# The first block of a two-block model as one program block: rows normalised after the projection, attention in the order three-branch, latent, banded

## What is computed

```python
def hybrid_layer(x, w_in, w_out, g_pre, g_post, ...):
    h = rms_norm(x, g_pre)
    a_q, a_kv, a_g, b_cq, b_ckv, b_kr, c_q, c_kv, z = split_cols(h @ w_in)
    o_a = nsa_attention(a_q, a_kv, a_g, cmp_pos, cmp_w1, cmp_w2, rel_bias[:4])
    qb = rms_norm(b_cq, q_norm) @ w_uq          # latent heads, rotary part added
    kvb = rms_norm(b_ckv, kv_norm) @ w_ukv
    o_b = causal_block_attention(q_full, k_full, v, scale)
    o_c = banded_attention(c_q, c_k, c_v, 128, rel_bias[4:], sinks)
    mixed = concatenate([o_a, o_b, o_c]) * silu(z)
    return x + rms_norm(mixed @ w_out, g_post)
```

## Time and profile before

| What | us |
|---|---|
| Median of three runs | 2661.77 (2660.51 to 2672.22) |
| The profiled execution | 2659.23, its span 2657.4 |
| First product of the input projection, layer 0 | 41.0 |
| Attention, layer 0 | 199.5 to 299.8 |
| Output projection, layer 0, last tile done | 353.5 |
| Input projection, layer 1, third tile starts | 395.0 |
| Second block's first instruction | 715.4 |

### The profile page before, as it was taken

How to read it: one execution, slowest core, us unless ns; L and a number is a source line. 1 busy time by engine, 2 the same in 40 slices (tenths; PEclk the granted TensorE clock), 3 DMA queues, 4 the chain that set the end, 5 groups by cost and what they waited for, 6 DMA issues and landing times. The chain is left out here.

```text
span 2657.4 us, 35733 instructions
## 1 busy us (share of the span) xinstructions
PE 2513.5 (95%) x13328; PEld 2002.8 (75%) x13328; DVE 1274.9 (48%) x1879; ACT 685.4 (26%) x1365; POOL 673.9 (25%) x516
## 2 busy tenths in 40 slices
PE   7999879998799999999899999899999999999997
PEld 4875558765488888787688888688887887788886
DVE  4446454465443334586733344433344876533344
ACT  2126431165221110354311110311100642311101
POOL 1006430064233321200433311233311101433311
PEclk9999989998899999998999999899999999999999
DMA  5310123200322332230233332233322321233322
GB/s 205 95 56 1 41 94 98 69 1 17 102 87 95 99 111 91 72 97 25 87 100 98 95 113 89 64 95 97 112 99 72 96 65 56 83 99 95 116 98 75
DMA packets 57556, 223.35 MB, mean 84 GB/s; under 512 B 6696, under 2 KB 7848, under 8 KB 57056
## 3 DMA queue, kind: packets, MB, share of 16 engines
q1 hardware_dynamic: 56000, 213.97, 25.0%
q10 hardware_dynamic: 1440, 7.79, 0.8%
HBM read 219.59 MB, written 2.15 MB: 83 GB/s over the span
## 5 line engine op out<-in xcount | busy, mean ns | idle before, releaser
L171 DVE CAST two_hi<-two_raw 128x1024 fp32r<-128x1024 f32 (+1 forms) x292 | 219.8, 753 | 907.6 <-PE bank L240 897.1
L233 PE MATMUL bank<-xh,two_hi 128*128 128x512 f32 x1728 | 429.8, 391 | 0.1
L240 PE MATMUL bank<-xl,two_hi 128*128 128x512 f32 x1728 | 427.5, 389 | 0.0
L236 PE MATMUL bank<-xh,two_lo 128*128 128x512 f32 x1728 | 426.8, 389 | 0.0
L173 DVE TENSOR_TENSOR two_lo<-two_raw,two_hi 128x1024 fp32r<-128x1024 f32 (+1 forms) x292 | 400.9, 1373 | 10.0
L236 PEld LDWEIGHTS bank<-xh,two_lo 128*128 128x128 f32 x1728 | 324.4, 188 | 67.6
L240 PEld LDWEIGHTS bank<-xl,two_hi 128*128 128x128 f32 x1728 | 324.4, 188 | 67.2
L233 PEld LDWEIGHTS bank<-xh,two_hi 128*128 128x128 f32 x1728 | 322.9, 188 | 68.6 <-issue 1.4
L1464 POOL TENSOR_TENSOR up_hm<-up_sg,up_hm 128x512 f32<-128x512 f32 x88 | 197.5, 2244 | 555.9 <-ACT up_hm L1446 555.9
L233 PE MATMUL bank<-hh,two_hi 128*128 128x512 f32 x704 | 171.8, 392 | 0.0
L240 PE MATMUL bank<-hl,two_hi 128*128 128x512 f32 x704 | 171.4, 390 | 0.0
(11 more groups left out here) (318 smaller groups left out, 3131.9 us busy)
## 6 DMA issues: line engine op xcount, KB each, us to landing
two_raw<-in_up SPq DMA_DIRECT2D x180, 512.0 KB, 3.5
two_raw<-in_down SPq DMA_DIRECT2D x64, 704.0 KB, 4.0
one_raw<-in_w_in SPq DMA_DIRECT2D x52, 512.0 KB, 3.6
two_raw<-in_w_in SPq DMA_DIRECT2D x40, 512.0 KB, 3.6
one_raw<-in_w_out SPq DMA_DIRECT2D x16, 512.0 KB, 3.5
two_raw<-in_w_out SPq DMA_DIRECT2D x16, 512.0 KB, 3.7
w<-in_w ACTq DMA_DIRECT2D x2, 2048.0 KB, 10.5
x<-in_x SPq DMA_DIRECT2D x1, 2048.0 KB, 8.3
```

The lines of the kernel that those rows point to most:

```text
L171: v.tensor_copy(st.hi[:, h, 0:w], st.raw[:, r, 0:w]).then_inc(st.hi_made, 1)
L233: pe.matmul(out[:], st.hi[:, slot, k * P:(k + 1) * P], xh[:, h * kp + k, :], start=h == 0 and k == 0, stop=False)
L236: pe.matmul(out[:], st.lo[:, slot, k * P:(k + 1) * P], xh[:, h * kp + k, :], start=False, stop=False)
L240: mm = pe.matmul(out[:], st.hi[:, slot, k * P:(k + 1) * P], xl[:, h * kp + k, :], start=False, stop=h == pieces - 1 and k == kp - 1)
```

## The change

- **One block.** `first_block` writes out both layers for each engine, without barriers or a loop; the loads of SyncE too (`fetch_first`).
- **Start.** x comes in four pieces with two weight tiles between. The distance rows are made after the first two tiles. Of the four far rows (4 × 1,024) and eight near rows (8 × 384) 128 copies each go to DRAM (`store_bias`, after the load of weight tile 7), and `read_bias`, after the load of tile 11, reads them back with a row step one shorter than the row, so that no turning is needed. `biasK` is gone: compressed keys read every sixteenth element of `biasA`.
- **Norm.** `xh` and `xl` are made of x times the gain, without the root. ScalarE squares x afterwards, VectorE adds the squares, TensorE sums them after tile 3, and VectorE multiplies with the root as it moves each tile out of PSUM (`evict`). Tiles 0 to 5 have six banks. SiLU is then a step of its own on ScalarE.
- **Attention.** The 24 three-branch pairs come first, then 8 latent, then 16 banded. At steps 17 and 20 VectorE splits the first two tiles of the output projection; in the last steps ScalarE (`convert`) and then GpSimd make `xh` and `xl` of the mixed rows.
- **Output projection.** Eight banks hold the result. ScalarE squares from PSUM, VectorE scales in place and adds to x, and layer 1 takes chunks of x as they are made. No second sum of squares is made here.

```diff
-            sp.dma_start(kit.x[:], d["x"]).then_inc(s["x_loaded"], 16)
-            kit.stream.start(sp)
-            sp.dma_start(d["scratch"], vec[:]).then_inc(s["stored"], 16)
...
-            sp.dma_start(ha[:], bass.AP(src.tensor, src.offset, [[1, P], [2 * T, A_HEADS], [1, 896]])
...
+def fetch_first(sp, st, n):
+    sp.dma_start(st.raw[:, u, :], src[at:at + 1].rearrange("o p k -> (o p) k")).then_inc(st.w_loaded[u], 16)
...
+        for i in range(4):
+            sp.dma_start(kit.x[:, 2 * i:2 * i + 2, :], d["x"][:, 2 * i:2 * i + 2, :]).then_inc(s[f"x_in{i}"], 16)
+            if i < 2:
+                fetch_first(sp, st, i)
...
+    def store_bias(sp):
+        sp.wait_ge(s["vec_made"], 3)
+        sp.dma_start(d["far"], first.vec[0:A_HEADS].unsqueeze(1).to_broadcast([A_HEADS, P, 2 * T])
+                     ).then_inc(s["stored"], 16)
+        sp.dma_start(d["near"], first.near[:].unsqueeze(1).to_broadcast([C_HEADS, P, NEAR_W])).then_inc(s["stored"], 16)
+    def read_bias(sp):
+        sp.wait_ge(s["stored"], 32)
+        for dst, name, sem, heads, w, n in ((kit.biasC, "near", "read_c", C_HEADS, NEAR_W, 256),
+                                            (kit.biasA, "far", "read_a", A_HEADS, 2 * T, BIAS_W)):
+            src = d[name]
+            sp.dma_start(dst[:], bass.AP(src.tensor, src.offset + P - 1, [[w - 1, P], [w * P, heads], [1, n]])
+                         ).then_inc(s[sem], 16)
...
 def attention_pairs():
+    for c in range(2):
+        for n in reversed(range(NT)):
+            for b, kind in enumerate(("cmp", "slc", "win")):
+                add(kind, c, n, (2 * c, 2 * c + 1), branch=b, first=b == 0, last=b == 2)
+    for c in range(2):
+        for n in reversed(range(NT)):
+            add("mla", 2 + c, n, (2 * c, 2 * c + 1), first=True, last=True)
-    for c in range(4):
-        for n in reversed(range(NT)):
-            add("swa", 4 + c, n, (2 * c, 2 * c + 1), first=True, last=True)
...
-    return (0, 4)[i % 2]
+SPLIT_AT = (17, 20)
+TILES = (0, 1, 2, 3, 4, 5, 6, 7)
+IN_BANKS = (0, 4, 1, 2, 6, 7)
+Y_BANKS = (0, 4, 1, 2, 6, 7, 3, 5)
+XSUM_BANK = 3
+    return IN_BANKS[i] if i < len(IN_BANKS) else IN_BANKS[(i - len(IN_BANKS)) % 4]
...
-            a.activation(kit.xrstd[:], kit.xsum[:], ACT.Ln, bias=kit.eps[:, 0:1], scale=1.0 / D).then_inc(s["ln_made"], 1)
-                a.activation(kit.xh[:, c, :], hn[:, c, :], ACT.Copy).then_inc(s["xhi_made"], 1)
-                v.scalar_tensor_tensor(hn[:, c, :], kit.x[:, c, :], kit.gpre[:, c:c + 1], kit.xrstd[:],
-                                       ALU.mult, ALU.mult).then_inc(s["hn_made"], 1)
+            gain = kit.gains[:, 0, l, c:c + 1]
+            a.activation(kit.xh[:, c, :], kit.x[:, c, :], ACT.Copy, scale=gain).then_inc(s["xhi_made"], 1)
+            a.activation(hn[:, c, :], kit.x[:, c, :], ACT.Copy, scale=gain).then_inc(s["hn_made"], 1)
+        for c in range(DC):
+            a.activation(xsq[:, c, :], kit.x[:, c, :], ACT.Square).then_inc(s["xsq_made"], 1)
+        a.dma_start(s1[:], d["s1"][l]).then_inc(s["s1_in"], 16)
...
+        a.activation(kit.xrstd[:], bank[XSUM_BANK][:], ACT.Ln, bias=kit.eps[:, 0:1], scale=1.0 / D
+                     ).then_inc(s["ln_made"], 1)
...
-            def evict(i):
-                a.wait_ge(st.mm_done, st.done_after(l, base + i))
-                a.activation(proj[:, i, :], bank[dense_bank(i)][:], ACT.Silu if i < C_Z + DC else ACT.Copy,
-                             scale=HD ** -0.5 if i in SCALED else 1.0).then_inc(s["out_taken"], 1)
+        def evict(i):
+            v.wait_ge(st.mm_done, n0 + i + 1 + HL_RING)
+            if i == 0:
...
+            if i in SCALED:
+                out = v.scalar_tensor_tensor(proj[:, i, :], src, HD ** -0.5, kit.xrstd[:], ALU.mult, ALU.mult)
+            else:
+                out = v.tensor_tensor(proj[:, i, :], src, kit.xrstd[:], ALU.mult)
+            out.then_inc(s["taken"], 1)
...
+                for c in range(1, DC):
+                    v.wait_ge(s["xsq_made"], c + 1)
+                    if c > 1:
+                        v.wait_ge(s["xsq_added"], c - 1)
+                    v.tensor_tensor(xsq[:, 0, :], xsq[:, 0, :], xsq[:, c, :], ALU.add).then_inc(s["xsq_added"], 1)
+            if i == 3:
+                for e in range(3):
+                    evict(e)
+            if i >= 3:
+                evict(i)
...
+            if j in SPLIT_AT:
+                split(N_IN + SPLIT_AT.index(j))
...
+        convert_at = {NU - 4: (0, 1), NU - 3: (2, 3), NU - 2: (4,), NU: (5,), NU + 1: (6,)}
+        def convert(p):
+            a.wait_ge(s["turned"], groups_of[NU - L_RING + p // 2][-1] + 1)
+            a.wait_ge(s["mixed"], p + 1)
+            a.activation(kit.xh[:, p, :], rows_of(p), ACT.Copy).then_inc(o["xhi_made"], 1)
...
+        for p in range(DC):
+            g.wait_ge(s["turned"], groups_of[NU - L_RING // 2 + p // 2][-1] + 1)
+            g.wait_ge(o["xhi_made"], p + 1)
+            g.tensor_tensor(kit.xl[:, p, :], rows_of(p), kit.xh[:, p, :].bitcast(F32), ALU.subtract
+                            ).then_inc(o["xlo_made"], 1)
...
-                a.activation(y[:, c, :], bank[c % 2][:], ACT.Copy).then_inc(s["out_taken"], 1)
-                v.scalar_tensor_tensor(y[:, c, :], y[:, c, :], kit.s1[:, S_GPOST + c:S_GPOST + c + 1], rs[:],
-                                       ALU.mult, ALU.mult).then_inc(s["scaled"], 1)
-                    v.tensor_tensor(kit.x[:, c, :], kit.x[:, c, :], y[:, c, :], ALU.add).then_inc(s["x_made"], 1)
-                a.activation(y[:, c, :], kit.x[:, c, :], ACT.Square).then_inc(s["xsq_made"], 1)
-                mm = pe.matmul(kit.xsum[:], kit.ones[:], y[:, c, :], start=c == 0, stop=c == last)
+            row = y[:, c, :] if c < Y_KEPT else bank[Y_BANKS[c]][:]
+            if c == 0:
+                v.wait_ge(s["y_kept"], Y_KEPT)
+            v.scalar_tensor_tensor(row, row, kit.gains[:, 1, l, c:c + 1], rs[:], ALU.mult, ALU.mult
+                                   ).then_inc(s["scaled"], 1)
+            v.wait_ge(s["scaled"], c + 1)
+            v.tensor_tensor(kit.x[:, c, :], row, kit.x[:, c, :], ALU.add).then_inc(s["x_made"], 1)
...
-            with nc.Fori(0, DEPTH) as l:
-                phase_attend(kit, l)
-                phase_out1(kit, l)
-            phase_leave(kit, ("start", "out1"))
+            first_block(kit)
...
+        layers = [(attend(kit, first, l, begin), project_out(kit, first, l)) for l in range(DEPTH)]
+        @block.tensor
+        def _(pe):
+            begin["tensor"](pe)
+            for att, out in layers:
+                att["tensor"](pe)
+                out["tensor"](pe)
```

More of the change, by code:

```diff
@@ L80 @@
 UNROLL = 4
+BIAS_W, NEAR_W = 896, 384
 LINE = 64
@@ L448, in add @@
         pairs.append(dict(kind=kind, tile=tile, n=n, heads=heads, **more))
-    for c in range(4):
-        for n in reversed(range(NT)):
-            add("swa", 4 + c, n, (2 * c, 2 * c + 1), first=True, last=True)
-    for c in range(2):
-        for n in reversed(range(NT)):
-            add("mla", 2 + c, n, (2 * c, 2 * c + 1), first=True, last=True)
     for c in range(2):
@@ L458, in attention_pairs @@
                 add(kind, c, n, (2 * c, 2 * c + 1), branch=b, first=b == 0, last=b == 2)
+    for c in range(2):
+        for n in reversed(range(NT)):
+            add("mla", 2 + c, n, (2 * c, 2 * c + 1), first=True, last=True)
+    for c in range(4):
+        for n in reversed(range(NT)):
+            add("swa", 4 + c, n, (2 * c, 2 * c + 1), first=True, last=True)
     for u in pairs:
@@ new lines, in weight_tile @@
+def weight_tile(pe, st, n, out, order, xh, xl):
+    slot = n % HL_RING
+    pe.wait_ge(st.hi_made, n + 1)
+    for k in range(DC):
+        w = order[k]
+        pe.matmul(out[:], st.hi[:, slot, w * P:(w + 1) * P], xh[:, k, :], start=k == 0, stop=False)
+    pe.wait_ge(st.w_split, n + 1 + RAW_RING)
+    for k in range(DC):
+        w = order[k]
+        pe.matmul(out[:], st.lo[:, slot, w * P:(w + 1) * P], xh[:, k, :], start=False, stop=False)
+    for k in range(DC):
+        w = order[k]
+        mm = pe.matmul(out[:], st.hi[:, slot, w * P:(w + 1) * P], xl[:, k, :], start=False, stop=k == DC - 1)
+    mm.then_inc(st.mm_done, 1)
@@ L867, in weigh @@
-            def weigh(x):
-                u = pairs[x]
-                tile = u["tile"]
-                out = bank[out_bank[tile]]
-                wait_copies(pe, groups_of[x][-1])
-                order = tiles_in_order.index(tile)
-                if order >= 2:
-                    pe.wait_ge(s["mixed"], order - 1)
-                for y in range(u["m"]):
-                    for hh in range(2):
-                        mm = pe.matmul(out[HD * hh:HD * hh + HD, u["n"] * P:(u["n"] + 1) * P],
-                                       values(u, hh, u["lo"] + y), pt(x)[0:u["rows"], hh, y * P:(y + 1) * P],
-                                       start=u["first"] and y == 0, stop=u["last"] and y == u["m"] - 1)
-                mm.then_inc(s["pv_mm"], 1)
```

(7 more changed lines are left out.)

1277 lines of the change are left out of this document (654 added, 623 removed).

## The result

The changed kernel takes 2677.4 us (median of 16 runs, 2670.1 to 2680.0), the kernel before 2665.8 us beside it (16 runs): ratio **1.0043, 95% interval 1.0033 to 1.0053**. That is 11.7 us slower, under the 0.5% named in the prediction, but a real difference, and 74 us above the 2603 that was forecast. It lies inside the stated range, 2585 to 2690.

The account below looks back on a forecast made before the run. TensorE's products were a floor, losses lying between first-block stages. Terms −27.5 + 5.0 − 19.6 + 9.0 − 21.0 − 3.2 = −57.3 from 2659.2 gave 2602, stated as 2603 us; range 2585 to 2690.

Parts of the forecast that it names:

- The bias store: Writing copied distance rows to DRAM behind weight tile 7: engines taken at full rate, hidden under TensorE's work, cost nothing.
- the mask row: Profiled load of the old mask, 12 rows of 4 KB: 23 GB/s per busy engine, taken as full rate.
- the prediction's own upper bound: Bias store if few source rows get one engine's share, 26 GB/s: far rows 80 us, near rows 30 us.
- Rival 1: Few source rows bound the store; weight tile 8 stalls 80 us, plus 2.5 us half clock: 2685 us; chance 0.35.
- Start −27.5: Start of the kernel to tile 2 of layer 0's input projection: begins at 27.9 instead of 55.68 us, −27.5 us.
- Inside the input projection +2.5 a layer: Evictions hidden by TensorE; an fp32 sum and late key copies on the path: +5.0 us for two layers.
- Attention +4.5 a layer: Two weight splits (1.5 to 2 us each) and eight copies (1 to 1.5 us) slow attention; order costs nothing: +9.0 us.
- Attention to output projection −9.8: Attention's end to the output projection's third tile: 11.2 instead of 21.0 us, 9.8 a layer, −19.6 us altogether.
- Layer 0 to 1 −21.0: Layer 0's last output tile to layer 1's third tile: second sum, barriers and scaled copies gone, −21.0 us.
- End of the block −3.2: Layer 1's last tile to the second block: no GpSimd additions, no second sum, one barrier less, −3.2 us.
- Second block, 0: Second block, not touched by the change: a floor, with no term in the sum, so 0 us.
- the four cases: Whole-kernel outcomes: forecast 0.53, few source rows binding 0.35, other engines binding 0.09, change doing less than claimed 0.03.

Follow-up runs that it names:

- run 2: Changed kernel with the same four far and eight near source rows placed four partitions apart instead of on neighbouring partitions: 2591.9 us, ratio 0.974.
- run 3: Run 2's layout with distance rows made four times over, all 16 far and 32 near copies read by the store: 2587.2 us, ratio 0.972.
- run 12: As run 2, but far rows on partitions 0, 32, 64, 96 and near rows 16 apart: 2625.0 us, ratio 0.986.
- run 5: Run 3's kernel with the two weight splits of attention made after its last step: 2610.7 us, ratio 0.982.
- run 6: Run 3's kernel with ScalarE's eight copies of xh made after attention instead of in its last steps: 2589.0 us, ratio 0.974.
- run 1: Changed kernel with distance rows made 32 (far) and 16 (near) times over, so the store reads 128 source rows: 2590.6 us, ratio 0.973.
- run 7: Run 3's kernel with attention back in the old order, banded, latent, then three-branch heads: 2600.7 us, ratio 0.977.
- run 9: Run 7's old attention order plus run 5's late weight splits, on run 3's kernel: 2614.8 us, ratio 0.982.

## Why the prediction was wrong

- **The bias store, taken at nothing: the step that failed.** It was argued from the mask row (12 rows of 4 KB, 23 GB/s for a busy engine) that few rows are served at full rate. 2 MB from four rows go at 26 GB/s in all, 6.5 an engine (stretch 32 to 64 us), and runs 2, 3 and 12 show the shared port. Mistaken was the row as much as the size: the mask row is a load into SBUF of 48 KB, and I extended it to a store of 3.7 MB out of SBUF. Its window of 0.25 us can't carry the reading either: the same view gives the windows 2.25 to 2.50 and 3.25 to 3.50 us of that trace DMA shares of 1.43 and 1.63, more than all engines can be busy. The Trainium skill's rule (SBUF — State Buffer, "Door 1: The DMA port swizzle"), which the prediction set beside it and didn't take, had the right side with an estimate of 106 us; the store took 113.6 us (30.0 to 143.66), and the prediction's own upper bound was 110.
- **Rival 1 was the case.** It put 80 us of stall at weight tile 8 and 2.5 us of half clock behind it: 81.0 us measured, at tile 8, and 3.75 us for the first eight products instead of 1.98, 1.9 us lost until the clock was back. Its total of 2685 was 8 us too high, since the rest of the sum came out 8 us better than forecast in this kernel (the profiled executions differ by 17.4, and 17.4 − 83 = −66 for the other stages, where −57 was said). Of these 8 us, 4.3 lie in the second block, of which the forecast said nothing: that part is luck.
- **Start −27.5:** −26.4. Tile 2 at 29.3 instead of 27.9, first product at 9.67 instead of 8.5. In run 3 with larger masks −24.3.
- **Inside the input projection +2.5 a layer:** in layer 1 +2.9 (run 3). The parts are there, 1.25 us for the keys (1.5 forecast) and 1.0 for the sum. In the changed kernel it is +6.2, where the granted clock stood lower (below); over all runs the same stage took 146.7 to 151.6 us. Layer 0 costs 2.4 us more in run 3, because tile 2 begins at half clock.
- **Attention +4.5 a layer: mis-sized.** Measured by the lengths 100.1 and 99.4 against 100.3 and 101.6, by the idle time 0.0 to 0.2 more a layer. Splits cost at most 1.0 instead of 3 to 4, the copies 0.3 to 1.1 instead of 1 to 1.5, and the order, costed at nothing, saves 2 to 3. In the old order with late splits the idle time is still 1.7 above that of before; the copies explain 0.3 to 1.1 of it, the rest is open.
- **Attention to output projection −9.8:** tile 2 stands 11.0 us behind attention's last product, where it was 21.0, and run 5 gives the 10 us back. Right. Without the early splits nothing is left of it (run 5); without the early copies 1 us of it goes (run 6: 12.0 instead of 11.0).
- **Layer 0 to 1 −21.0:** −22.2. **End of the block −3.2:** −3.2.
- **Second block, 0:** −4.3 (−7.1 in run 3). One VectorE gap at a layer's border, "issue" in the profile, is 7.8 us in the profile of before and 3.5 to 3.8 in that of the changed kernel and of all twelve runs. Nothing in the records says what filled it, and there is one profile of before only. Before, then after:

```profile
DVE x L1225 <- issue: 7.8, 1, 7.8
...
DVE x L1340 <- issue: 3.5, 1, 3.5
```


- **In the prediction's figures:** this block has 1,536 weight products (2 layers × 32 tiles × 24) and not 3,456; no term uses it. Its shares of the four cases give about 0.61 for faster, 0.12 for same and 0.26 for slower, where 0.63, 0.10 and 0.27 are written.

The sum of the stages without the hole is −72 (run 3) against the −57 of the forecast. Attention is 12.7 us better than forecast, the second block 7.1 and the way from layer 0 to 1 1.2; the start and the input projections take 6.4 back.

## What to carry to other kernels

Count the ports under a transfer's SBUF rows, not its bytes or its engines: four rows on neighbouring partitions moved 26 GB/s, the same four rows 4 partitions apart 107, and moving them made the start 1.5 us longer (run 2). A slow transfer costs first what stands behind it in its queue, then the engine that issues it when much of it is still waiting on few DMA engines (34 us twice here), then whoever waits for its semaphore; each has to be followed before it is put anywhere. And when an effect is below 4 us, compare stages by TensorE's idle time rather than by their length, and only between profiles with a like busy time: here the idle time of one and the same code moved by 0.9 us.

## What had not been expected of the hardware

- A DMA issue can hold its engine while the transfer before it is still waiting: issuing the near store took 34.3 us on SyncE and 34.9 us on ScalarE, 8.4 in run 2 and 15.7 in run 12. It is not the slowness alone: in run 3 the far store moved 104 GB/s, no faster than in run 2, and the issue took 0.6 us, as in run 1. What differs is that the far store gives 128 rows of 4 KB to each of four DMA engines in the held cases, and 32 to each of sixteen in runs 1 and 3. Where it was held, each engine had moved about the same by then: 34.25 us at 26/4, 8.39 at 107/4 and 15.72 at 50/4 GB/s are 223, 224 and 197 KB, some 50 rows (an estimate). So a limit on what may wait at each DMA engine fits all runs; none was made to test it.
- The granted clock differs from run to run in the same stage. The same stretch, 74.5 us behind tile 2 of layer 1, first in the changed kernel, then in run 3:

```profile
500.00:540.00 40.00, 40.00 (x173) 31.11 (x172) 18.31 (x27) 6.69 (x11) 0.00 (x0) 0.91 0.24 79
```

```profile
417.00:457.00 40.00, 40.00 (x180) 31.21 (x179) 18.32 (x27) 6.69 (x11) 0.00 (x0) 0.96 0.24 79
```

  TensorE is busy throughout both; the half-speed products lie in and right behind the 32 narrow ones (31 columns) that compress the keys. The layer's input projection took 151.6 us in the one and 148.3 in the other, and run 7 and run 3 differ in the same way. So of the 12 us between the profiles of runs 7 and 3, 3 us lie in a stage that its edit doesn't touch; run 9, with the same order, has 148.3 there.
